# Block 2's gate matmuls ahead of its attention, beside index scores and projections

## The reference, cut to what matters

```
hn = rms_norm(h);  proj = hn @ w_in                       # aq ak av bq bkv iq ik iw gates (2 x 1024 wide)
gate_a, gate_b = split(sigmoid(gates + b_gates))
o_a = sliding_window_sink_attention(aq, ak, av)            # 8 heads, "A" below
score = sum_h relu(iq_h @ ik) * iw_h;  sel = top 128 of score per query      # 4 index heads
o_b = attention of (rms_norm(bq) @ w_uq) over the selected rows of rms_norm(bkv)   # 8 heads, "B" below
h = h + (gate_a * (o_a @ w_branch_a) + gate_b * (o_b @ w_branch_b)) @ w_out
h = h + (silu(rms_norm(h) @ w_gate) * (rms_norm(h) @ w_up)) @ w_down
```

## Time and profile before

| | |
|---|---|
| median of 3 runs | 1692.31 us (1691.06 to 1700.18) |
| profiled execution, own time | 1703.56 us |
| its span, first to last instruction | 1701.8 us |
| busy: TensorE, VectorE, ScalarE, GpSimd | 1581.7, 828.4, 616.0, 359.2 us |
| mean granted TensorE clock | 0.945 |
| HBM read, written | 138.32, 5.36 MB |

### The profile page before, as it was taken

How to read it: one execution, slowest core, us unless ns; L and a number is a source line. 1 busy time by engine, 2 the same in 40 slices (tenths; PEclk the granted TensorE clock), 3 DMA queues, 4 the chain that set the end, 5 groups by cost and what they waited for, 6 DMA issues and landing times.

```text
span 1701.8 us, 19427 instructions
## 1 busy us (share of the span) xinstructions
PE 1581.7 (93%) x7174; PEld 1255.3 (74%) x7178; DVE 828.4 (49%) x1588; ACT 616.0 (36%) x1132; POOL 359.2 (21%) x434
## 2 busy tenths in 40 slices
PE   6899988899999999999998877779999999999995
PEld 5787665588877888888886755448887788888884
DVE  5446554444444333433458796334444443443444
ACT  5433455522234222322454455433223322222222
POOL 3200643400020000000136346540002120120112
PEclk9899778999999999999999877789999999999998
DMA  5734100233322333333324600022332233333321
GB/s 188 131 90 129 57 1 13 66 107 99 99 84 77 99 97 91 97 100 99 94 87 110 114 13 1 7 87 87 99 100 87 87 97 92 96 99 99 100 78 59
DMA packets 41918, 145.47 MB, mean 85 GB/s; under 512 B 5170, under 2 KB 5362, under 8 KB 41824
## 3 DMA queue, kind: packets, MB, share of 16 engines
q1 hardware_dynamic: 37088, 128.98, 24.4%
q0 software_dynamic: 4736, 15.25, 4.4%
HBM read 138.32 MB, written 5.36 MB: 84 GB/s over the span
## 4 chain that ended last, share of the span: by engine, by line
PE 83%; DVE 8%; ACT 4%; issue 3%; DMA 1%; POOL 1%; DVEq 0%; SPq 0%; ACTq 0%; POOLq 0%
PE PSA L494 81%; PE PSA L659 2%; ACT AR L1119 1%; PE PSA L789 1%; DVE AR L1553 1%; DVE AR L1551 1%; DVE WL L1463 1%; DMA WR<-w_in 0%; DVE AR L1969 0%; DVE ARR L1559 0%; DVE PSA L1501 0%; DVE AR L1666 0%; ACT AR L1130 0%; ACT AR L1169 0%; DVE AR L1578 0%
## 5 line engine op out<-in xcount | busy, mean ns | idle before, releaser
L494 PE MATMUL PSA<-Ah,WH 128*128 128x512 f32 x1072 | 430.3, 401 | 21.7 <-DVE WL L1463 21.7
L494 PE MATMUL PSA<-Al,WH 128*128 128x512 f32 x1072 | 424.0, 395 | 0.0
L494 PE MATMUL PSA<-Ah,WL 128*128 128x512 f32 x1072 | 423.6, 395 | 0.0
L1047 ACT CAST WH<-WR 128x1024 fp32r<-128x1024 f32 (+3 forms) x233 | 239.7, 1032 | 237.1 <-PE PSA L494 236.0
L1463 DVE TENSOR_TENSOR WL<-WR,WH 128x1024 fp32r<-128x1024 f32 (+3 forms) x223 | 269.4, 1209 | 97.6 <-ACT WH L1047 97.3
L494 PEld LDWEIGHTS PSA<-Ah,WH 128*128 128x128 f32 x1072 | 205.4, 192 | 69.1 <-issue 22.7
L494 PEld LDWEIGHTS PSA<-Ah,WL 128*128 128x128 f32 x1072 | 205.3, 191 | 43.9
L494 PEld LDWEIGHTS PSA<-Al,WH 128*128 128x128 f32 x1072 | 205.5, 192 | 43.0 <-issue 0.7
L494 PE MATMUL PSA<-Bh,WH 128*128 128x512 f32 x584 | 226.6, 388 | 2.2 <-DVE ARR L1559 2.2
L494 PE MATMUL PSA<-Bh,WL 128*128 128x512 f32 x584 | 226.5, 388 | 0.0
L494 PE MATMUL PSA<-Bl,WH 128*128 128x512 f32 x576 | 224.1, 389 | 0.0
(11 more groups left out here) (357 smaller groups left out, 2010.5 us busy)
## 6 DMA issues: line engine op xcount, KB each, us to landing
WR<-w_in SPq DMA_DIRECT2D x228, 512.0 KB, 3.5
WR<-w_in SPq DMA_DIRECT2D x8, 384.0 KB, 3.1
XT<-scr_tmp POOLq DMA_DIRECT2D x8, 264.0 KB, 12.8
XT<-xT_in SPq DMA_DIRECT2D x4, 512.0 KB, 8.4
XT<-scr_tmp POOLq DMA_DIRECT2D x8, 256.0 KB, 13.4
XT<-xT_in POOLq DMA_DIRECT2D x1, 2048.0 KB, 10.1
x_tmp<-XT POOLq DMA_DIRECT2D x1, 2048.0 KB, 9.0
XT<-x_tmp POOLq DMA_DIRECT2D x1, 2048.0 KB, 9.3
```

Source lines behind the costliest of these rows:

```text
L494: return pe.matmul(o, l, r, start=start, stop=stop)
L1047: ac.copy(WH[p][:, 0:n], WR[j % RAW][:, 0:n]).then_inc(w_hi, 1)
```

## The change

Block 2's 16 gate tiles move from the merge to the stretch ahead of attention. The first eight go one half tile (12 matmuls) into each of the 16 steps of the index loop; `bq`, which was there, goes before the transposes. The other eight stand between `ak`, the `aq` tiles, `uq` and `ukv`. Their low halves are made by GpSimd. ScalarE copies each gate's bank to one of five buffers GO, and SP writes it to DRAM. For the merge SP reads them back into four buffers G2, GpSimd multiplies by the reciprocal root (before: VectorE in PSUM), ScalarE takes tanh, and VectorE does (tanh + 1) x branch in one instruction; the factor 0.5 is applied when the sum is split. In block 1's merge the last two hold too, and GpSimd's 0.5 x + 0.5 goes.

Attention 2's buffers that lay in WW lie in AHL, the place of the input halves Ah and Al, which nothing needs once the gates are made. So the tiles br2 0 to 2 can be split before and during attention. The top operations have a new order: five in each index step from step 4 on, always of the row with the most left, the remaining ones between the projections, none in attention. Several semaphores are merged into shared ones with stages.

```diff
+    g = [(f"g{'ab'[n % 2]}2", n // 2, 1024, True) for n in range(16)]
+    t += g[0:8] + [("ak", 0, 1024, True), g[8], aq[0], g[9], aq[1], g[10], aq[2], g[11], aq[3], g[12], g[13]]
+    t += [("uq", 0, 1024, True), g[14], ("ukv", 0, 1024, True), g[15]]
+    t += [("br2", i, 1024, True) for i in range(8)]
-    pool_lo = ("bkv", "bq", "ak", "aq", "uq", "ukv")
+    pool_lo = ("bkv", "bq", "ak", "aq", "uq", "ukv", "ga2", "gb2")
+        GO = [AR[:, c:c + 512] for c in (3168, 3680, 4224, 4736, 17152)]
+        G2 = [AHL[:, 6144 + 512 * i:6656 + 512 * i] for i in range(4)]
+        for n in range(28):
+            ready, left = [qt for qt in (3, 2, 1, 0) if n >= 4 * (4 - qt)], {}
+            for m in range(5 if n < 16 else 128):
+                left = {qt: 32 - sum(q == qt for q, c in top_seq) for qt in ready}
+                qt = max(ready, key=lambda q: (left[q] * SCw[q], q), default=None)
+                if qt is not None and left[qt]:
+                    top_seq.append((qt, 32 - left[qt]))
+            top_by.append(len(top_seq))
 # SP
+            def gate_out(n):
+                sp.wait_ge(g_ev, n + 1)
+                sp.dma_start(d["gt"][n, :, :], GO[n % 4 if n < 15 else 4]).then_inc(d_go[n % 4 if n < 15 else 4], 16)
+            def gate_in(n):
+                if n < 4:
+                    sp.wait_ge(w_mm, mm_no[gate_tile(15)])
+                else:
+                    sp.wait_ge(m_dv.sem, m_dv.at(2, 3 * (n // 2 - 2) + n % 2))
+                s = n % 4 if n < 15 else 4
+                sp.wait_ge(d_go[s], 16 * (n // 4 + 1 if n < 15 else 1))
+                sp.dma_start(G2[n % 4], d["gt"][n, :, :]).then_inc(d_gi[n % 4], 16)
+            out_at = {gate_tile(n) + 7: n for n in range(16)}
+            in_at = {tid["br2", i] + 5: i for i in range(2, 8)}
 # TensorE, index loop
-                if n % 8 == 0:
-                    ws = halves_ready(tid["bq", n // 8])
-                last = chunk(ws, hA, n % 8, bank(n // 8), 8)
+                if n % 2 == 0:
+                    ws = halves_ready(gate_tile(g))
+                    if g > 1:
+                        pe.wait_ge(g_ev, g - 1)
+                for k in range(4 * (n % 2), 4 * (n % 2) + 4):
+                    last = chunk(ws, hA, k, bank(gate_bank(g)), 8)
 # TensorE, after the loop: gate(n) is feat(gate_tile(n), hA, 8, bank(gate_bank(n)))
+            gate(8)
+            feat(tid["aq", 0], hA, 8, bank(AQB[0]))
+            pe.wait_ge(g_ev, 7)
+            gate(9)
...
+            gate(12)
+            pe.wait_ge(g_ev, 10)
+            gate(13)
             wh, wl = halves_ready(tid["uq", 0])
...
+            pe.wait_ge(g_ev, 13)
+            gate(14)
             wh, wl = halves_ready(tid["ukv", 0])
...
             latent_values(4, bank(2)[0:NM, :])
+            pe.wait_ge(h_lo.sem, h_lo.at("kb", 1))
+            gate(15)
+            pe.wait_ge(g_ev, 16)
             attention2()
 # TensorE, merge, block 2: the first two branch tiles, a halves first
+                        pe.wait_ge(r_lo, 7)
+                        branches(0, (0,))
+                        branches(1, (0,))
+                        pe.wait_ge(r_lo, 8)
+                        branches(0, (1,))
+                        branches(1, (1,))
 # ScalarE (the last three lines come before its first write of KBA)
+            def gate_out(n):
+                s = n % 4 if n < 15 else 4
+                result(gate_tile(n))
+                if 3 < n < 15:
+                    ac.wait_ge(d_go[s], 16 * (n // 4))
+                ac.copy(GO[s], bank(gate_bank(n))).then_inc(g_ev, 1)
+                split_to(gate_tile(n) + 3)
+                    if p + w == 0:
+                        for s in range(4):
+                            ac.wait_ge(d_go[s], 64 if s < 3 else 48)
 # VectorE, attention2 (ScalarE has the first two lines too)
+                    if t == U2 // 2:
+                        split_to(tid["br2", 2])
                     if t == 32:
                         top_run(128)
+                        dv.wait_ge(d_go[4], 16)
 # VectorE, merge
-                        dv.wait_ge(m_sg.sem, m_sg.at(ph, 2 * i + w))
-                        dv.tensor_tensor(T1[sl], GS[sl], bank(2 + w + 4 * (i % 2)), ALU.mult).then_inc(m_dv.sem, 1)
+                        dv.wait_ge(m_th.sem, m_th.at(ph, 2 * i + w))
+                        dv.scalar_tensor_tensor(out=T1[sl], in0=(GS if ph == 1 else G2)[sl], scalar=1.0, in1=bank(branch_banks(ph, i)[w]),
+                                                op0=ALU.add, op1=ALU.mult).then_inc(m_dv.sem, 1)
 # GpSimd, block 2's merge
+            for n in range(16):
+                pl.wait_ge(d_gi[n % 4], 16 * (n // 4 + 1))
+                pl.tensor_tensor(G2[n % 4], G2[n % 4], RBG[2], ALU.mult).then_inc(g_sc, 1)
```

More of the change, by code:

```diff
@@ L113, in sem @@
             return ctx.enter_context(nc.semaphore(name))
+        with nc.sbuf_tensor("AHL", [128, 16 * T], F) as AHL:
+            pass
         Ah, Al = sb("Ah", [128, 8, T], R), sb("Al", [128, 8, T], R)
@@ L457, in build, with gate_tile, gate_bank, branch_banks @@
         index_of = [(qt, h) for qt in (3, 2, 1, 0) for h in range(4)]
[L458 to L462, removed]
+        top_seq, top_by = [], []
+        for n in range(28):
[6 more added lines that the diff above has]
+            top_by.append(len(top_seq))
+        def gate_tile(n):
+            return tid["ga2" if n % 2 == 0 else "gb2", n // 2]
+        def gate_bank(n):
+            return n % 2 if n < 8 else (4, 0, 6, 4, 3, 0, 3, 5)[n - 8]
+        def branch_banks(ph, i):
+            b = 2 + (4 if ph == 1 else 2) * (i % 2)
+            return b, b + 1
+        AQB, UQB, VBB = (5, 1, 7, 2), (5, 1, 6, 4), (7, 2, 0, 3)
         def sync_program(sp):
@@ L590, in merge, with branches @@
                 ga, gb, br, wo = names
[L591 to L595, removed]
-                    wh, wl = halves_ready(tid[br, i])
[L597 to L604, removed]
+                def branches(i, ws):
+                    wh, wl = halves_ready(tid[br, i])
+                    bb = branch_banks(ph, i)
+                    for w in ws:
                         for k in range(4):
@@ L610, in merge @@
                             last = mm(bank(bb[w]), c, Bh[:, kk, :], False, k == 3)
-                    last.then_inc(w_mm, 1)
+                    if 1 in ws:
+                        last.then_inc(w_mm, 1)
+                for i in range(8):
+                    if ph == 1:
+                        for w, nm in ((0, ga), (1, gb)):
+                            if i > 1:
+                                pe.wait_ge(m_th.sem, m_th.at(ph, 2 * (i - 2) + w))
+                            feat(tid[nm, i], hA, 8, bank(w + 4 * (i % 2)))
+                    if i == 0 and ph == 1:
+                        pe.wait_ge(p_lo, 8)
+                    elif i == 0:
+                        pe.wait_ge(r_lo, 7)
[4 more added lines that the diff above has]
+                        branches(1, (1,))
+                    if i > 1:
+                        pe.wait_ge(m_dv.sem, m_dv.at(ph, 3 * (i - 2) + 1))
+                    if i > 1 or ph == 1:
+                        branches(i, (0, 1))
                 def ready(k):
@@ L927, in tensor_program @@
             feat(tid["bkv", 0], hA, 8, bank(6), om=bank(7)[:, 0:NM])
+            pe.wait_ge(e_d.sem, e_d.at("ik", 3))
+            for i in range(2):
+                feat(tid["bq", i], hA, 8, bank(4 + i))
             pe.wait_ge(i_ln, 12)
@@ L990, in tensor_program @@
                     pe.wait_ge(e_a.sem, e_a.at("vb", 0))
-                for o, x0, x1 in ((bank(2 + i), 0, T), (bank(6)[:, NM * i:NM * i + NM], T, TM)):
+                for o, x0, x1 in ((bank(UQB[i]), 0, T), (bank(7)[:, NM * i:NM * i + NM], T, TM)):
                     mm(o, a, ckh[:, x0:x1], True, False)
@@ L1956, in vector_program @@
             dv.tensor_copy(IK[:, 0:NM], bank(1)[:, 0:NM]).then_inc(e_d.sem, 1)
+            for i in range(2):
+                result(tid["bq", i])
+                dv.tensor_tensor(bqr[:, i, :], bank(4 + i), rb[:, 0:T], ALU.mult).then_inc(e_d.sem, 1)
             for n, (qt, h) in enumerate(index_of):
```

418 lines of the change are left out of this document (229 added, 189 removed).

## The result

The changed kernel takes 1682.53 us (median of 14 runs, 1678.57 to 1690.59), the kernel before on the same chip 1691.68 (14 runs, 1690.0 to 1702.4): a ratio of 0.9938, 95% interval 0.9919 to 0.9958. That is 9 us faster; 30 were predicted. The profiled executions took 1703.56 and 1689.02 us. They stand 14.5 apart, more than the medians, because the one of before was among that kernel's slower ones.

The account below looks back on a forecast made before the run. TensorE, busy 93% of the span, was taken to bound the kernel. Terms -87.1 + 12.3 + 25.4 + 26.2 - 8 + 5 - 4 = -30.2 us gave 1673.4 profiled, 1662 median; range 1647 to 1684.

Parts of the forecast that it names:

- Part 6: Attention's end: the 2.97 us wait for the first cast and low half goes, with some half-clock matmul cost; -4 us.
- Part 1: Merge: 16 gate tiles of 5.44 us leave, all on the path; -87.1 us.
- Part 2: Before the index scores: two bq tiles, transposes and VectorE's copies and scalings come first; loop starts 12.3 us later.
- Part 3: Index loop: eight gate tiles added, VectorE mostly setting the pace; 61 us in place of 35.6, +25.4.
- The lock that I allowed 3 us for: Index loop: GpSimd's low halves exclude VectorE's two-input additions; 3 us added.
- Rival A: Index loop: the lock meets every two-input instruction of steps 4 to 15, +22 less 3; 1681 us, chance 0.15.
- Part 4: From ak to attention: eight gates added and a new 4 us wait before gate 15; 90.6 us, +26.2.
- Part 5: Attention: first half -8 without top operations; step 32's masks wait for gate 15, +4 (0 to 7); ScalarE's casts +1.
- Part 7: Merge's new load: engine work per tile and the gates' return from DRAM cost 0, ends 0 and +13 us.
- Rival B: Merge: the gates' return sets the pace, with crowded transfers of 8.4 us, +13 to 15; 1676 us, chance 0.09.
- Part 8: Block 1's merge: GpSimd steps go, VectorE instructions change form at the same 0.69 us, TensorE runs unbroken; 0.
- the 11.25 us that the prediction carried over: Whole kernel: median of runs 11.25 us below the profiled execution; the same difference taken for the changed kernel.

Follow-up runs that it names:

- before again: The kernel before, unedited, run again on a third chip for a second trace: 1694.74 us, ratio 1.0001.
- after again: The changed kernel, unedited, run again on another chip: 1683.05 us, ratio 0.9922 to the kernel before.
- three edits: Changed kernel with low halves at attention step 16, gate 14's transfer straight behind gate 13's, casts ahead of block 2's tanh waits: 1662.56 us, ratio 0.9813.
- sixteen places: Changed kernel with all 16 of block 2's gate tiles given places of their own on return from DRAM: 1681.57 us, ratio 0.9939 to the kernel before.

## Why the prediction was wrong

By stages, in us. The first column of numbers is the first trace of before, on which the sum stood.

| stage | before | before again | predicted | after | after again | three edits |
|---|---|---|---|---|---|---|
| start to loop | 906.3 | 898.2 | 918.6 | 918.1 | 914.2 | 916.0 |
| loop to attention | 100.0 | 99.6 | 151.6 | 154.0 | 155.5 | 148.9 |
| attention | 134.1 | 130.2 | 127.1 | 134.2 | 134.8 | 125.5 |
| merge to the 1.33 us wait | 145.7 | 145.7 | 58.6 | 65.2 | 63.5 | 56.0 |
| rest | 415.8 | 415.8 | 415.8 | 415.8 | 415.8 | 415.8 |

(Part 6's 4 us is counted in attention in the column predicted; about 2.6 of it belongs in the merge.)

- **Part 1**, 16 x 5.44 off the merge: right. With casts in the better order the branch phase is 56.0, that is 145.7 less 89.7: the 87.1, and the cold matmuls of part 6.
- **Part 2**, +12.3: right. The first traces give 11.8; the means of two and ten traces give 914.05 - 902.25 = 11.8.
- **Part 3**, a loop of 61 us: 59.14. The size was right, the reason wrong. VectorE was to set it, and TensorE does, busy 58.66 us; with the gates almost out it took 54.6. The lock that I allowed 3 us for is there: see below. Rival A did not come.
- **Part 4**, 90.6 from ak to attention with a new wait of 4: it was 94.8, and the wait of 3.36 stood where it was said, for that reason, and went with the order of one transfer. Mis-sized was what follows a wait: the low level of the clock, 1.4 us here. The sum had put gate 15 at the warm pace and kept the cold one as an end only. Without the wait the stretch is 88.8, where my terms without it give 86.6; no run says which of them is 2.2 too small.
- **Part 5**, attention. First half -8: -6.6, from where it was said. Step 32, +4 with a span of 0 to 7: it stalled 7.6 us, past the upper end. The mechanism was right to the engine and the transfer. But the 4 us that TensorE was to work on before it needed the masks were 2.2 (1110.33 to 1112.50), and the transfer to DRAM, for which I took the 3.6 of a lone load, took 5.50 beside weight loads of 512 KB. The second half, without the wait of 2.97, should have been 84.1 us and was 86.1, at clock 0.77 in place of 0.81; that is less than the 4.5 by which two executions of the kernel before differ there (87.1 and 82.6), so it says nothing about the change.
- **Part 6**: right; the merge starts with no wait.
- **Part 7**, the merge's new load, 0 with ends 0 and +13: **the step that failed as a step.** It cost 6.7 and 5.0 us of holes in two traces, and 9.2 and 7.5 of branch phase against the kernel with the casts first; the difference goes with the clock, 0.97 against 1.00 in the first of them. I had added up the load of each engine (VectorE 4.0 and ScalarE 3.0 of 5.44 us a tile) and the length of the gates' return, and both were small enough. (The terms that I wrote for the return add up to 10.0 us, not 11.8, which changes nothing here.) The prices were not at fault either: a gate's load took 4.1 us in the median, against 3.6, and a product of GpSimd 1.29, against 2.13. I had also written that SP's waits hold back only loads that are needed 20 us later. What I did not do is read ScalarE's program in order: the cast of tile i+2 stands behind two tanh that wait for gates, and that of branch tile 3 comes a round late besides, so a late gate, which nobody needs yet, stops the weight that TensorE needs. An engine busy 24.93 of 65.21 us [the stretches above] stopped one that should never wait. Rival B named the gates' return and gave 1676; its place was right, but its cause, a crowded transfer, was not: more places did not help, and another order did, with the same transfers.
- **Part 8**: right; block 1 ended as before.

The miss against the first trace is 15.5 us: parts 2 and 3 gave 2.4 back, part 4 cost 4.2, attention 7.1 (first half 1.4, step 32 with the casts 2.7, second half 3.0), the merge 6.6. The rest to the 20 between the medians is that the trace of before stood 11 above its median, and the one of after only 6.5 above its own: the 11.25 us that the prediction carried over belonged to one execution, not to the kernel.

With the three waits gone the median is 1662.56, and 1662 was forecast. That they meet is in part luck. The forecast held 8 us of waits (4 before gate 15, 4 at step 32) that this kernel doesn't have; without them it would have been 1654, and the 11.25 us carried over, where this kernel's trace stood 1.4 above its median, make up for them. Trace against trace it is 1671.7 - 8 = 1663.7 us of span, and 1662.2 was measured: the sum of the work was right to some 2 us. What failed is the price of the order in the queues: the wait before gate 15 lacked the low clock behind it, the one at step 32 was put at about half, and the merge's were put at nothing.

## What to carry to other kernels

When a step moves, write out each engine's program in order around its new place, and ask of each waiting instruction what stands behind it, and whether the bottleneck needs that sooner. Loads added up per engine don't show this. A transfer that gives a buffer free belongs in the queue as soon as its data exist, not behind loads that wait for something else. And price a new wait of a few us on TensorE with the low clock behind it. Last, a difference of a few us between two single traces can be the spread of executions; take a second trace of the kernel before, too.

## What the runs showed of the hardware

- The lock between VectorE and GpSimd inside the loop of the changed kernel: VectorE's additions, and GpSimd's low half beside the second.

```profile
939.78 0.63 DVE L2122 SCALAR_TENSOR_TENSOR AR<-AR 128x400 f32<-128x400 f32 x1 [0.48 <-ACT AR L1485]
944.79 2.70 DVE L2122 SCALAR_TENSOR_TENSOR AR<-AR 128x400 f32<-128x400 f32 x1
```

```profile
944.68 2.37 POOL L2248 TENSOR_TENSOR WL<-WR,WH 128x1024 fp32r<-128x1024 f32 x1 [1.72 <-ACT WH L1146]
```

The addition that came 0.11 us after GpSimd's start took 2.70 us in place of 0.63 and ended 0.44 after GpSimd's end, 947.05. It was held, not slowed. The Trainium skill (SBUF — State Buffer, Who interferes with whom) calls the port pair that the two engines share an exclusive lock, and says of VectorE's two-port modes that whoever issues first keeps it for the whole instruction and the other fully blocks. The trace agrees, for an addition with two inputs in SBUF.

- Whether a hole costs the clock as well differs, and not by its length alone. In the changed kernel the next matmuls started 0.23 us apart behind 1.82 us at 1224.67, and 0.43 apart behind 3.36 us at 1064.03. Behind 3.13 us before gate 15, with the low halves at step 16, the first started at the fast pace and the later ones 0.43 apart. Behind 2.40 us in the merge with sixteen places they started 0.43 apart at once, though TensorE had been busy 11.81 of 12.20 us at clock 1.00 before it.
- Gate 15's 256 KB to DRAM took 5.50 us beside loads of 512 KB; the changed kernel's 16 such transfers took 2.0 to 14.6 us, with a median of 4.5. A lone load of 256 KB took 3.6, but on another queue and in the other direction, so the cost of the neighbours alone is not shown.
